# Hybrid decoder trunk on one core: a new order of the five weight blocks of a head, and a head's token mixing that starts within its own round

## The reference, cut to what matters

```python
xa, ga, qb, fb, ib, gb = jnp.split(u, ...)
xc = conv_b + sum(xpad[:, j:j+T] * cw[j] for j in range(4))   # recurrent input, convolved
a, bt from sigmoid gates of xc;  hs = scan(a * h + bt);  y_a = hs * gelu(ga)
q = silu(qb) * 128**-0.5;  f = lb + (1-lb)*sigmoid(fb);  k = (1-lb)*sigmoid(-fb);  v = ib
o, S = _hgrn2(q, k, v, log f, S0)              # gated linear recurrence, 4 heads of 128
y_b = rms(o) * gn * silu(gb)
x = x + concat(y_a, y_b) @ w_out;  x = x + square(relu(rms(x) @ w_up)) @ w_down;  y = rms(x)
```

## Time and profile before

| | |
|---|---|
| median of 3 runs | 2554.12 us (2553.91 to 2554.99) |
| profiled execution | 2556.64 us, its span 2555.0 us |
| PE busy | 2463.9 us, 96% of the span |
| DVE busy | 969.5 us, 38% |
| ACT busy | 618.9 us, 24% |
| chain that ended last, by engine | PE 92%, DVE 5%, ACT 2% |

### The profile page before, as it was taken

The page is one execution under the profiler, slowest core; times in us unless marked ns, Lnnn a source line. Parts: engine busy times, 40 slices in busy tenths (PEclk is TensorE's granted clock), DMA queues, the critical chain, the costliest instruction groups (busy, mean ns, idle before and its releaser), DMA issues.

```text
span 2555.0 us, 33915 instructions
## 1 busy us (share of the span) xinstructions
PE 2463.9 (96%) x13514; PEld 2212.7 (87%) x13514; DVE 969.5 (38%) x1587; ACT 618.9 (24%) x1149; POOL 283.9 (11%) x276
## 2 busy tenths in 40 slices
PE   5999999999999999999899999999999999999995
PEld 4778877878888888888798998999999999999995
DVE  6665764332121121123765665554211211211224
ACT  4243244222031121122323123232200200200211
POOL 0000001212212222222100000000000000000000
PEclk9999999999999999999999999999999999999998
DMA  5322234434444344444422222142223232222323
GB/s 190 104 94 95 84 100 165 146 124 141 134 146 148 128 143 148 144 160 176 125 104 67 67 66 81 60 152 74 91 83 99 82 98 83 88 93 82 99 82 106
DMA packets 86622, 284.34 MB, mean 111 GB/s; under 512 B 14096, under 2 KB 17296, under 8 KB 86544
## 3 DMA queue, kind: packets, MB, share of 16 engines
q1 hardware_dynamic: 41472, 151.01, 17.7%
q0 software_dynamic: 27648, 100.68, 12.1%
q10 hardware_dynamic: 17424, 31.57, 3.5%
HBM read 171.54 MB, written 111.68 MB: 111 GB/s over the span
## 4 chain that ended last, share of the span: by engine, by line
PE 92%; DVE 5%; ACT 2%; issue 1%; ACTq 1%; DVEq 0%
PE bank L419 28%; PE bank L421 28%; PE bank L420 28%; PE aux L479 3%; PE aux L552 1%; PE aux L468 1%; DVE a_lo L1237 1%; PE aux L508 1%; ACT s_in L617 1%; PE aux L531 1%; PE aux L530 1%; DVE xc L1195 1%; PE aux L484 1%; DVE xy L971 0%; PE aux L432 0%
## 5 line engine op out<-in xcount | busy, mean ns | idle before, releaser
L419 PE MATMUL bank<-a_hi,w_hi 128*128 128x358 f32 (+2 forms) x2560 | 925.5, 362 | 37.6 <-DVE a_lo L1237 20.5
L421 PE MATMUL bank<-a_hi,w_lo 128*128 128x358 f32 (+2 forms) x2560 | 908.7, 355 | 0.0
L420 PE MATMUL bank<-a_lo,w_hi 128*128 128x358 f32 (+2 forms) x2560 | 908.4, 355 | 0.0
L419 PEld LDWEIGHTS bank<-a_hi,w_hi 128*128 128x128 f32 x2560 | 485.8, 190 | 89.9 <-POOL w_lo L374 22.6
L421 PEld LDWEIGHTS bank<-a_hi,w_lo 128*128 128x128 f32 x2560 | 486.5, 190 | 46.2
L420 PEld LDWEIGHTS bank<-a_lo,w_hi 128*128 128x128 f32 x2560 | 486.3, 190 | 45.5 <-issue 1.5
L419 PE MATMUL bank<-b_hi,w_hi 128*128 128x512 f32 (+2 forms) x1280 | 453.2, 354 | 0.0
L420 PE MATMUL bank<-b_lo,w_hi 128*128 128x512 f32 (+2 forms) x1280 | 452.8, 354 | 0.0
L421 PE MATMUL bank<-b_hi,w_lo 128*128 128x512 f32 (+2 forms) x1280 | 452.3, 353 | 0.0
L1324 DVE TENSOR_TENSOR xy<-xy,bank 128x356 f32 (+3 forms) x160 | 94.5, 591 | 564.5 <-PE bank L421 564.5
L374 POOL TENSOR_TENSOR w_lo<-w_st,w_hi 128x1024 fp32r<-128x1024 f32 x74 | 180.2, 2435 | 1034.1 <-ACT w_hi L617 1034.1
(11 more groups left out here) (156 smaller groups left out, 1503.7 us busy)
## 6 DMA issues: line engine op xcount, KB each, us to landing
w_st<-in_wall SPq DMA_DIRECT2D x96, 512.0 KB, 4.2
kept_hi<-w_hi SPq DMA_DIRECT2D x96, 512.0 KB, 4.9
kept_lo<-w_lo SPq DMA_DIRECT2D x96, 512.0 KB, 5.7
w_hi<-kept_hi POOLq DMA_DIRECT2D x96, 512.0 KB, 3.8
w_lo<-kept_lo POOLq DMA_DIRECT2D x96, 512.0 KB, 4.6
xs<-in_xT ACTq DMA_DIRECT2D x8, 536.0 KB, 7.2
xy<-in_xT ACTq DMA_DIRECT2D x8, 536.0 KB, 7.1
xs<-in_xT ACTq DMA_DIRECT2D x16, 256.0 KB, 6.5
```

The lines of the kernel that those rows point to most:

```text
L419: pe.matmul(ps, wh, xh, start=(j == 0), stop=False)
L420: pe.matmul(ps, wh, xl, start=False, stop=False)
L421: mm = pe.matmul(ps, wl, xh, start=False, stop=(j == 7))
```

## The change

The order of blocks in a round becomes recurrent input, value, forget, query, output gate. The weights in memory keep their place; SP loads the first 20 blocks through a table. `GATE` moves to slot 13 in pass 0 and slot 16 in pass 1. The chain of head `i` starts in its own round, at slot 16 in pass 0 and 24 in pass 1, that is, with the output gate's block, and goes on in round `i+1`. In pass 0 `VT`, `D`, `L1`, `L2` are in slots 16 to 19 and `L3` to `L7`, `KT`, `U`, `O`, `R`, `N`, `OT`, `Y` in slots 0, 1, 2, 3, 4, 5, 6, 8, 9, 10, 11, 12 of the next round. In pass 1 `VT`, `D`, `L1`, `L2`, `L3` are in slots 24, 26, 27, 28, 29 and `L4`, `L5`, `L6`, `L7`, `KT`, `U`, `O`, `R`, `N`, `OT`, `Y` in slots 1, 2, 4, 5, 6, 7, 9, 10, 11, 13, 14. The masked values and new states get a buffer of their own (`s_stage`, the second half of `w_st`, which is free in pass 1). Cut to its core:

```diff
-V, G, XA, F, Q = range(5)
+XA, V, F, Q, G = range(5)
+STORED = [2, 0, 3, 4, 1]
+POST = {F: 0, Q: 1, G: 2}
-SLOTS = [dict(zip(range(16), PIECES)),
-         dict(zip([0, 4, 5, 6, 8, 9, 10, 12, 13, 14, 15, 16, 18, 19, 21, 22], PIECES))]
-GATE_SLOT = [16, 24]
+CHAIN_START = [16, 24]
+SLOTS = [dict(zip([16, 17, 18, 19, 20, 21, 22, 23, 24, 25, 26, 28, 29, 30, 31, 32], PIECES)),
+         dict(zip([24, 26, 27, 28, 29, 31, 32, 34, 35, 36, 37, 39, 40, 41, 43, 44], PIECES))]
+GATE_SLOT = [13, 16]
...
-                    if i >= 1 and s in SLOTS[p]:
-                        pieces.append((SLOTS[p][s], i - 1))
+                    if i >= 1 and s < CHAIN_START[p] and s + 10 * NT[p] in SLOTS[p]:
+                        pieces.append((SLOTS[p][s + 10 * NT[p]], i - 1))
                     if i < HEADS and s == GATE_SLOT[p]:
                         pieces.append(("GATE", i))
+                    if i < HEADS and s >= CHAIN_START[p] and s in SLOTS[p]:
+                        pieces.append((SLOTS[p][s], i))
...
+        s_stage = w_st[:, 1, :].rearrange("p (a d) -> p a d", a=2)
...
+            for n in range(GA0):
+                sync.wait_ge(w_ready, n + 1)
+                load(stored_at(n + 2), n % 2)
+                keep(n, n % 2)
...
                 elif name[0] == "L" and int(name[1]) >= DIRECT:
+                    drained(act, AUX[(p, f"L{DIRECT - 1}", i)])
...
-                    elif kind == Q:
-                        act.wait_ge(post, post_no(p, 0, it, NT[p] - 1) + 1)
-                        if p and it > 0:
-                            act.wait_ge(s_store, 16 * it)
+                    elif kind == G:
+                        act.wait_ge(post, post_no(p, POST[Q], it, NT[p] - 1) + 1)
                     elif it > 0:
-                        act.wait_ge(post, post_no(p, 2, it - 1, NT[p] - 1) + 1)
+                        act.wait_ge(post, post_no(p, POST[G], it - 1, NT[p] - 1) + 1)
...
-                    dve.wait_ge(post, post_no(p, 0, min(i + 1, HEADS - 1), NT[p] - 1) + 1)
-                    vm = tmp[0:T8, :, :].rearrange("p a (b d) -> p (a b) d", d=P)
+                    dve.wait_ge(w_ready, BLOCKS)
+                    vm = s_stage[0:T8, :, :].rearrange("p a (b d) -> p (a b) d", d=P)
...
                 elif name == "Y":
+                    dve.wait_ge(post, post_no(p, POST[G], i, NT[p] - 1) + 1)
```

More of the change, by code:

```diff
@@ L346, in load, with stored_at @@
                 sync.dma_start(w_st[:, slot, :], wall[m]).then_inc(w_in[slot], 16)
+            def stored_at(n):
+                return n // 5 * 5 + STORED[n % 5] if n < GA0 else n
             def keep(m, slot):
@@ L352, in _ @@
             for j in range(2):
-                load(j, j)
-            with sync.Fori(0, BLOCKS // 2 - 1) as i:
+                load(stored_at(j), j)
+            for n in range(GA0):
+                sync.wait_ge(w_ready, n + 1)
+                load(stored_at(n + 2), n % 2)
+                keep(n, n % 2)
+            with sync.Fori(GA0 // 2, BLOCKS // 2 - 1) as i:
                 for j in range(2):
@@ L462, in piece @@
                     for t in range(NT[p]):
-                        pe.wait_ge(post, post_no(p, 2, i, t) + 1)
+                        pe.wait_ge(post, post_no(p, POST[Q], i, t) + 1)
                     for s, (c, m) in enumerate(chunk_sets(p)):
@@ L513, in piece @@
                         for s in range(2):
-                            pe.matmul(open_bank(a + 3 + s)[:, :], k_tok[0:T8, 8, :], tmp[0:T8, s, :],
+                            pe.matmul(open_bank(a + 3 + s)[:, :], k_tok[0:T8, 8, :], s_stage[0:T8, s, :],
                                       start=True, stop=True).then_inc(aux_done, 1)
@@ L744, in piece @@
                             drained(act, AUX[(p, "U", i)] + s)
-                        act.dma_start(ssn_d[i], tmp[:, :, :]).then_inc(s_store, 16)
+                        act.dma_start(ssn_d[i], s_stage[:, :, :]).then_inc(s_store, 16)
                 elif name == "N":
@@ L778, in unit_fn @@
                 if kind in (G, Q):
-                    pn = post_no(p, 0 if kind == G else 2, it, t)
+                    pn = post_no(p, POST[kind], it, t)
                     evacuated(act, u)
@@ L1035, in piece @@
                     filled(dve, a + 1 + p)
-                    dve.wait_ge(post, post_no(p, 2, i, NT[p] - 1) + 1)
+                    dve.wait_ge(post, post_no(p, POST[Q], i, NT[p] - 1) + 1)
                     tt(q[:, 0:th], q[:, 0:th], f[:, 0:th], ALU.mult).then_inc(level, 1)
@@ L1084, in piece @@
                         tot = f[:, NP[1] + SLEN - 1:TH[1]:SLEN].rearrange("p (b o) -> p b o", o=1)
-                        new = tmp[:, :, :].rearrange("p a (b d) -> p (a b) d", d=P)
+                        new = s_stage[:, :, :].rearrange("p a (b d) -> p (a b) d", d=P)
                         tt(new, s_smp[:, :, :], tot.broadcast_to([P, NSEQ, P]), ALU.mult).then_inc(s_step, 1)
@@ L1088, in piece @@
                         for s in range(2):
-                            tt(tmp[:, s, :], tmp[:, s, :], aux[(a + 3 + s) % 4][:, :], ALU.add).then_inc(
+                            tt(s_stage[:, s, :], s_stage[:, s, :], aux[(a + 3 + s) % 4][:, :], ALU.add).then_inc(
                                 aux_free[(a + 3 + s) % 4], 1)
@@ L1162, in finish_unit @@
                     return
-                pn = post_no(p, {G: 0, F: 1, Q: 2, None: 3}[kind], it if it < HEADS else blk - GA0, t)
+                pn = post_no(p, POST[kind] if kind is not None else 3, it if it < HEADS else blk - GA0, t)
                 dve.wait_ge(act_fn, pn + 1)
```

## The result

The changed kernel takes 2601.61 us in the median (2596.68 to 2602.46, 4 runs) against 2554.55 us (2553.91 to 2555.38, 4 runs) of the kernel before: ratio 1.018, 95% interval 1.0162 to 1.0198, slower by 47 us where +43.5 were forecast (2598). Its profiled execution took 2601.89 us, with a span of 2600.2 us: 45.2 us more than the span before.

What follows compares the result with a forecast made beforehand. PE, busy 96% of the span, was taken to bound the kernel. Waits of +27.3 us and clock of +16.8 make +44.1, from 2556.6 to 2600.7 profiled, about 2598 in the median; range 2571 to 2611.

Steps and rivals of the forecast that it cites:

- Step 1: L7 of pass 0: with the convolution in front of a merge, PE waits 3.8 us, three times, +11.3 us.
- Step 2: KT of pass 1: read-out and convolution precede the merge of L7; PE waits 5.2 us, three times, +15.6 us.
- Step 3: D of pass 0: PE waits 3.1 instead of 2.0 us, four times, +4.2 us; no cost at D of pass 1.
- Step 4: First round of pass 1: DVE runs behind; PE waits at a bank and a gate product, +5.4 us, bounds 0 and 8.
- Step 5: Waits that go away: all at OT, -8.7 us, and at the output projection of pass 0, -0.5 us.
- The clock: Low granted clock on PE behind eleven gaps over 3 us, 2.3 us each, 25.3 less today's 8.5: +16.8 us.
- the spared clock: Rival: the eleven gaps hardly slow PE's clock, so only +18.8 us, 2573 us; chance 0.10.
- the hidden convolution: Rival: DVE is through before PE needs the merges at L7 and KT; +3.4 us, 2557.5 us; chance 0.04.
- the other side: Rival: DVE's lateness never reaches PE, and D and OT lose their waits too; -18 us, 2536 us; chance 0.06.
- more is late than I see: Rival: D in pass 1 or a second wait for weights is late too; +16 us, 2613 us; chance 0.10.

Runs made afterwards that it cites:

- first experiment: The changed kernel with the convolution done one tap per slot, each behind the slot's piece, instead of in one go; 2556.07 us, ratio 1.0002.
- last experiment: The changed kernel with taps one per slot behind the pieces, GATE of pass 1 at slot 17, pass 0's D to U one slot later; 2531.16 us, ratio 0.9908.
- second experiment: The changed kernel with GATE of pass 1 at slot 17 instead of 16; 2596.4 us, ratio 1.0162.
- half-in-front: The changed kernel with only two of four convolution taps in front of the merge, the others behind it, one per slot; 2575.16 us, ratio 1.0075.
- the kernel with the later query: The kernel before with one more, unread DVE instruction of 1.2 us ahead of the scan in pass 0; 2563.08 us, ratio 1.0032.

## Why the prediction was right

**Step 1, `L7` of pass 0.** Forecast 3.8 us three times, measured 3.58. The first experiment, which changes only the place of the taps, removes it. Shown.

**Step 2, `KT` of pass 1.** Forecast 5.2, measured 5.15 three times; removed by the same experiment. Shown.

**Step 3, `D`.** Forecast 3.1, measured 3.02; the slack of a slot in the last experiment leaves 0.3. No wait at `D` of pass 1, as forecast. The same step missed something, though: with `GATE` at slot 16 the scan also holds up the read-out of the forget gate's third tile, and its bank is wanted at slot 24, since only the three query units lie between. That is +3.0 us, shown by `GATE` at slot 17. I had checked the query's way and not this bank.

**Step 4, first round of pass 1.** Forecast 4.6 at the gate product and 0.8 at a bank, together 5.4; measured 4.0 and nothing. The place and the mechanism are right (a `GATE` one slot later waits 2.9), the term is 1.4 us too large.

**Step 5, what goes away.** `OT`: all 8.7 us, as forecast. The output projection of pass 0: forecast -0.5, measured 0.0 (8.4 before and after). The pieces `Y` no longer precede it, but POOL's split does, and the first `a_lo` cannot end sooner.

**The clock.** Forecast 25.3 us in the changed kernel, from eleven gaps at 2.3; by the same count they lost 28.7, so 2.6 each, and the filled gaps show 27 us for ten of them. The mechanism is right and the term some 3 us low. Over the kernel before, the rest of the span is 16.7 us against my 16.8; the count of clock rows gives 20.2, so the close match is in part luck. So is the 2.3: it is a mean over gaps of 1.8 to 5.5 us, and gaps of 3.0 us lost anything from nothing to 3.1. The Trainium skill (TensorE: Matmul & The Clock Gate, section "HAM oscillation") warns of just this, that a kernel pays at each of a row of gaps; by the experiment with filled gaps the runs here agree, with 27 us for ten gaps of 3.0 to 5.2 us; in other versions some gaps of 3.0 us cost nothing.

Of the rivals, the spared clock is out by the filled gaps, the hidden convolution and the other side by the rows of waits. Of "more is late than I see" a small part is there, the three bank waits of 1.0 us, without a low clock behind them; `D` of pass 1 is not late. The sum was nonetheless helped by errors that cancel: 3.0 us left out and 0.5 that did not go away in step 5, against 1.4 too much in step 4 and 0.2 too long for each wait of step 1. The waits came to +28.5 us where 27.3 were forecast.

## What to carry to other kernels

When a block of work moves in a hand-written order, look at each engine's list for what now stands in front of an instruction that another engine waits for. Add the work in front, and compare it with the time the other engine needs to get there: here 7.4 against 3.6 us. A long piece of work without a deadline of its own (a convolution wanted ten slots later) should be cut up and put behind the short ones that have one. On PE count on average a gap of 3 us or more at some 1.7 times its length, as here: in ten of them, 38.3 us of waits and 27 us of clock.

## What the runs showed of the hardware

**A filled gap costs less than an idle one.** Products without a use, put into a wait, made the kernel 27 us faster, because the granted clock stayed at 1.0.

**A gap's price varies.** Behind gaps of 3.0 us at `D` the clock fell in 12 of 16 cases over four kernels (4 of 4 in the changed kernel, 3, 2 and 3 of 4 in the first, second and half-in-front experiments), with 1.4 to 3.1 us lost in ten us; behind the 3.2 us of the kernel with the later query it fell in 4 of 4; behind 3.6 us or more it fell each time, in 12 of 12 (three `L7` and three `KT` each in the changed kernel and in the second experiment). Behind single gaps of 0.9 or 1.0 us it never fell, behind two gaps of 1.3 and 1.2 to 1.5 us some 8 us apart it did, in all three heads. Behind the one bank wait of 2.8 us before the `rs` wait it fell in 2 of 8 profiles, the kernel before and its copy with the later query.

**From run to run the time goes with the granted clock.** The changed kernel's four runs took 2596.68 us at a mean granted clock of 0.980 and 2601.34 to 2602.46 at 0.976; `GATE` at slot 17 took 2590.29 at 0.980 and 2596.06 to 2596.81 at 0.976; the last version 2529.29 at 0.991 and 2534.78 at 0.988.
